# Keys of the cached sequences in pieces of two pages through four slots, 52 units for each sequence, and the sampled rows' pass between the prompt's last units

## The reference

```python
def project(x, w_in, b_f):                 # q, k, v (8 heads of 64), logf, u
    h = jnp.einsum('bsd,dc->bsc', x, w_in)
...
def fox_sample(q, k_new, v_new, logf_new, cache_k, cache_v, cache_logf, page_table):
    k_past = cache_k[page_table].reshape(DB, P, N_HEADS, HEAD_DIM)
    v_past = cache_v[page_table].reshape(DB, P, N_HEADS, HEAD_DIM)
...
    s = jnp.einsum('bqhd,bkhd->bhqk', q, k_all, preferred_element_type=jnp.float32) * HEAD_DIM ** -0.5
    s = s + (Fh[..., P:, None] - Fh[..., None, :])
...
    p = jax.nn.softmax(s, axis=-1)
    out = jnp.einsum('bhqk,bkhd->bqhd', p.astype(v_all.dtype), v_all)
...
def finish(x, attn, pool, w_o, ln1_g, ln1_b, w_gate, w_up, w_down, ln2_g, ln2_b):
    mix = jnp.einsum('bsc,cd->bsd', jnp.concatenate([attn.astype(x.dtype), pool.astype(x.dtype)], axis=-1), w_o)
    x1 = layer_norm(DEEPNORM_ALPHA * x + mix, ln1_g, ln1_b)
    hid = jax.nn.silu(jnp.einsum('bsd,df->bsf', x1, w_gate)) * jnp.einsum('bsd,df->bsf', x1, w_up)
    ffn = jnp.einsum('bsf,fd->bsd', hid, w_down)
    return layer_norm(DEEPNORM_ALPHA * x1 + ffn, ln2_g, ln2_b)
```

## Time and profile before

| | |
|---|---|
| median of three executions | 1519.34 us |
| the profiled execution | 1522.9 us, its span 1520.7 us |
| mean granted clock of TensorE | 0.947 of full |
| TensorE busy | 1384.2 us (91%) |
| VectorE, ScalarE, GpSimd busy | 737.0 (48%), 354.6 (23%), 534.7 us (35%) |
| moved by the DMA engines | 252.90 MB, 166 GB/s in the mean |
| read from HBM | 241.89 MB |

### The profile page before, as it was taken

The page is one execution under the profiler, slowest core; times in us unless marked ns, Lnnn a source line. Parts: engine busy times, 40 slices in busy tenths (PEclk is TensorE's granted clock), DMA queues, the critical chain, the costliest instruction groups (busy, mean ns, idle before and its releaser), DMA issues.

```text
span 1520.7 us, 21098 instructions
## 1 busy us (share of the span) xinstructions
PE 1384.2 (91%) x7585; PEld 1097.4 (72%) x7585; DVE 737.0 (48%) x1014; ACT 354.6 (23%) x514; POOL 534.7 (35%) x203
## 2 busy tenths in 40 slices
PE   7999999999984879999999999999899999998774
PEld 5898989988884867767767677777677777756422
DVE  4745354444659653545354745553554442225702
ACT  3534343533400232021211111212111112112300
POOL 1110000022134327456467365664564652120500
PEclk9999999999997989999999999999999999999756
DMA  7312011010553337666766577666575763424895
GB/s 248 108 56 70 28 57 41 29 49 1 169 191 105 128 116 231 228 199 192 242 191 222 171 246 229 198 225 218 175 230 190 243 248 112 152 106 147 302 347 211
DMA packets 103175, 252.90 MB, mean 166 GB/s; under 512 B 12576, under 2 KB 13985, under 8 KB 97688
## 3 DMA queue, kind: packets, MB, share of 16 engines
q1 hardware_dynamic: 99776, 240.68, 47.7%
q0 software_dynamic: 3296, 10.88, 2.1%
HBM read 241.89 MB, written 9.86 MB: 166 GB/s over the span
## 4 chain that ended last, share of the span: by engine, by line
PE 78%; DVE 10%; DMA 5%; issue 3%; ACT 2%; POOL 1%; SPq 0%; DVEq 0%; ACTq 0%; POOLq 0%
PE PSM L1261 30%; PE PSM L1279 15%; PE PSM L1031 11%; PE PSM L1301 4%; PE PSM L1097 4%; DMA AR<-ws 4%; PE PSM L1044 3%; PE PSM L1083 2%; PE PSM L1207 2%; PE PSM L1350 1%; PE PSM L1363 1%; DVE SC L1600 1%; PE PSM L1240 1%; DMA WR<-xT 1%; PE PSM L1378 1%
## 5 line engine op out<-in xcount | busy, mean ns | idle before, releaser
L681 POOL TENSOR_TENSOR AR<-AR,QB 128x2048 f32<-128x2048 f32 x64 | 300.2, 4699 | 121.7 <-DMA AR<-cache_k 109.1
L688 POOL TENSOR_TENSOR WL<-WR,WH 128x1024 fp32r<-128x1024 f32 x55 | 136.0, 2473 | 336.7 <-ACT WH L899 336.7
L1261 PE MATMUL PSM<-XH,WH 128*128 128x512 f32 x672 | 216.6, 404 | 0.0
L1261 PE MATMUL PSM<-XL,WH 128*128 128x512 f32 x672 | 212.8, 398 | 0.0
L1261 PE MATMUL PSM<-XH,WL 128*128 128x512 f32 x672 | 212.6, 398 | 0.0
L1600 DVE TENSOR_REDUCE SC<-AR 128x32 f32<-128x2048 f32 x64 | 145.8, 2279 | 109.8 <-POOL AR L681 109.8
L1787 DVE TENSOR_TENSOR ACC<-ACC,PSM 128x512 f32<-128x512 f32 x176 | 118.3, 683 | 133.6 <-PE PSM L1279 133.4
L1261 PEld LDWEIGHTS PSM<-XH,WH 128*128 128x128 f32 x672 | 123.4, 189 | 48.8 <-issue 22.2
L899 ACT CAST WH<-WR 128x1024 fp32r<-128x1024 f32 x55 | 57.5, 1047 | 413.6 <-PE PSM L1261 212.0
L1279 PE MATMUL PSM<-R 128*128 128x512 f32 x528 | 150.4, 393 | 0.0
L1261 PEld LDWEIGHTS PSM<-XH,WL 128*128 128x128 f32 x672 | 127.6, 190 | 30.4
(11 more groups left out here) (245 smaller groups left out, 2143.2 us busy)
## 6 DMA issues: line engine op xcount, KB each, us to landing
AR<-cache_k SPq DMA_DIRECT2D x256, 256.0 KB, 3.4
AR<-cache_v SPq DMA_DIRECT2D x256, 256.0 KB, 3.4
AR<-ws SPq DMA_DIRECT2D x37, 1024.0 KB, 7.1
WR<-ffn SPq DMA_DIRECT2D x66, 512.0 KB, 4.3
WR<-w_in SPq DMA_DIRECT2D x16, 512.0 KB, 3.7
WR<-w_o SPq DMA_DIRECT2D x5, 1024.0 KB, 5.1
WR<-xT SPq DMA_DIRECT2D x8, 512.0 KB, 5.6
AR<-negF_d SPq DMA_DIRECT2D x8, 512.0 KB, 3.8
```

Of the source, the lines that this page charges most:

```text
L681: pool.tensor_tensor(keys, keys, QB[:].rearrange("p (o n) -> p o n", o=1).to_broadcast([P, CH, AW]), ALU.mult).then_inc(k_mul, 1)
L688: pool.tensor_tensor(lo, WR[:, raw_weight(e), :], hi.bitcast(F32), ALU.subtract).then_inc(ffn_lo, 1)
L1261: ins = pe.matmul(out[:, hc], (hi, lo)[a][:, k * P:(k + 1) * P], x[b][:, k, hc], start=(k == 0 and n == 0), stop=(k == KC - 1 and n == 2))
```

## The change

Keys come in pieces of two pages (`KP`), 16 for each sequence, through four slots of half the size (`KS`), in the same memory. Multiplications and reductions are by piece, twice as many and half as long. In the output stage reductions stand behind products 8 to 22, and on SyncE four pieces are queued before the fourth load of output weights, and the first four pieces of sequence 1 before the wait for `vs_zero`. The sampled rows are turned before the mixer's last tile, and their mixer columns are made after product 1. Windows have 52 units; the two value slots are refilled at separate units. The sampled rows' layers begin at unit 418. Their G and U tiles are merged: a GU tile holds the same number of bytes, two row chunks for both, and leaves gate and up sums in one PSUM bank, so that one copy by ScalarE and half as many passes of TensorE sum them (with a mask `gumask` of 16 columns). There are 37 tiles as before, spaced 2 or 3 units, the last at 521; the rows' second layer norm stands at units 523 to 525. The FFN of the prompt, its units and the weight tiles are the same.

```diff
+KP = 2
+NKP = NPAGE // KP
+KS = 4
...
-KRED0 = {7: 0, 9: 1, 11: 2, 13: 3, 15: 4, 17: 5, 19: 6, 21: 7}
-WIN = 62
+KRED0 = {8: (0,), 9: (1, 2), 10: (3,)} | {n: (n - 7,) for n in range(11, 23)}
+WIN = 52
...
-VALUES = (9, 24, 39, 54)
-VLOAD = tuple(o + 2 for o in VALUES)
-OWN, COLUMNS, MAXIMUM, KEEP, HEADMAX = 57, 59, 60, 60, 61
-KMUL = (3, 10, 16, 23, 29, 36, 42, 49)
-KRED = tuple(o + 4 for o in KMUL)
-KLOAD = (0, 1) + tuple(o + 1 for o in KRED[:-2])
-ROWMAX, Q_LOAD, G_LOAD = 55, 53, 57
+VALUES = (9, 21, 32, 44)
+VLOAD = tuple(o + n for o in VALUES for n in (1, 4))
+OWN, COLUMNS, MAXIMUM, KEEP, HEADMAX = WIN - 5, WIN - 3, WIN - 2, WIN - 2, WIN - 1
+KMUL = tuple(2 + (WIN - 16) * i // (NKP - 1) for i in range(NKP))
+KRED = tuple(o + 3 for o in KMUL)
+ROWMAX, Q_LOAD, G_LOAD = WIN - 9, KMUL[-1] + 3, WIN - 6
...
+        order += [("GU", g, r) for r in range(parts("GU", g))]
+        order += [("D", g - 1, r) for r in range(parts("D", g - 1))] if g >= 1 else []
+    order += [("D", TGROUPS - 1, r) for r in range(parts("D", TGROUPS - 1))]
+    units = {step: TSTART + 5 * n // 2 + 3 * (n >= parts("GU", 0)) for n, step in enumerate(order)}
+    return units, [units["GU", g, parts("GU", g) - 1] + 2 for g in range(TGROUPS)]
...
+CSPAD = NB * WIN
+MIX, RESID, SQRT1, SCALE1, FACTORS1, OFFSETS1 = (CSPAD + n for n in (2, 11, 12, 13, 14, 18))
+TURN1, TURNED1, TSTART = (CSPAD + n for n in (20, 21, 22))
...
+SUNIT = {("W", n, 0): MIX + 2 * n for n in range(4)} | STEPS_S
+SAMPLE2 = max(SUNIT.values()) + 2
+LNVEC2 = BEGIN["D", NPAIR - 1] - 4
+LAST = max(SAMPLE2 + 5, NORM2 + 2 * RT + 4)
...
-        KR = [AR[:, n * 2 * D:(n + 1) * 2 * D] for n in (0, 1)]
+        KR = [AR[:, n * D:(n + 1) * D] for n in range(KS)]
...
-            first_keys(0)
-            first_keys(1)
+            keys(0)
+            keys(1)
             output_load_raw(2)
             sp.wait_ge(sn_st, 16 * 4)
             sp.wait_ge(ob_free, O["sw"] + 1)
             sp.wait_ge(tb_free, T["un"] + 1)
             sp.dma_start(QB[:], q_d[0:1, :].to_broadcast([P, AW])).then_inc(qb_ld, 16)
+            sp.wait_ge(lnew_done, 1)
+            keys(2)
+            keys(3)
+            output_load_raw(3)
             sp.wait_ge(g_st, 16 * NB)
             sp.dma_start(GB[:].rearrange("p t h -> p (t h)"), G_d[0]).then_inc(gb_ld, 16)
-            output_load_raw(3)
...
+            for n in range(12, NKP):
+                keys(n)
+            sp.wait_ge(k_mul, NKP)
             sp.dma_start(QB[:], q_d[1:2, :].to_broadcast([P, AW])).then_inc(qb_ld, 16)
+            for n in range(NKP, NKP + KS):
+                keys(n)
...
-                for c in range(NCH):
-                    n = (b + 1) * NCH + c
-                    if o == KLOAD[c] and b + 1 < NB:
-                        pages(n, KR, n % 2, t["cache_k"], k_ld, k_red, n - 1)
+                for i in range(NKP):
+                    n = (b + 1) * NKP + i + KS
+                    if o == KRED[i] + 1 and n < NB * NKP:
+                        keys(n)
...
-                    if o == VLOAD[c // 2 - 1] and n < NB * NCH:
+                    if o == VLOAD[c - 2] and n < NB * NCH:
...
             turn_pair(PAIRS - 1)
+            turn_sample(0)
+            turn_sample(1)
...
-                if n in (0, 2):
-                    turn_sample(n // 2)
-                if n == HRT - 1:
+                if n == 0:
                     sample_mixer()
...
-                    rounds = ((r, 0),) if cols == HALF else ((0, 0), (1, 4 * cols))
-                    for k, at in rounds:
+                    rounds, last = (1, 3) if cols == HALF else (2, 1)
+                    for a in range(rounds):
                         for q in range(4):
...
-                if n in (0, 2):
-                    keep_sample(n // 2)
-                if n == HRT + 1:
+                if n == 1:
+                    sample_columns()
                     sample_inputs()
...
+                if u == SAMPLE2:
+                    dve.wait_ge(t_used, len(STREAM))
+                    sample_mean(2, e_var)
+                if u == SAMPLE2 + 2:
+                    sample_scale(2)
+                    dve.wait_ge(e_vec_ld, 32)
+                    sample_factors(e_g1)
+                    dve.wait_ge(e_g1, 2)
+                    sample_offsets(xs2, svec2, e_y)
```

More of the change, by code:

```diff
@@ L138, in sample_steps, with parts @@
 def sample_steps():
[L140 to L141 removed]
     order = []
     for g in range(TGROUPS):
[L145 to L154, removed]
+        order += [("GU", g, r) for r in range(parts("GU", g))]
[3 more added lines that the diff above has]
+    return units, [units["GU", g, parts("GU", g) - 1] + 2 for g in range(TGROUPS)]
+def parts(kind, g):
+    full = 4 * g + 4 <= FT
+    return {"GU": (2, 4), "D": (1, 2)}[kind][full]
+CSPAD = NB * WIN
+MIX, RESID, SQRT1, SCALE1, FACTORS1, OFFSETS1 = (CSPAD + n for n in (2, 11, 12, 13, 14, 18))
+TURN1, TURNED1, TSTART = (CSPAD + n for n in (20, 21, 22))
+STEPS_S, SUMS = sample_steps()
+STREAM = [("W", n, 0) for n in range(4)] + list(STEPS_S)
 TINDEX = {step: n for n, step in enumerate(STREAM)}
[L156 removed]
+SUNIT = {("W", n, 0): MIX + 2 * n for n in range(4)} | STEPS_S
 NORM2 = BEGIN["D", NPAIR - 1] + 2
[L158 removed]
+SAMPLE2 = max(SUNIT.values()) + 2
+LNVEC2 = BEGIN["D", NPAIR - 1] - 4
+LAST = max(SAMPLE2 + 5, NORM2 + 2 * RT + 4)
 def weight_order():
@@ L415, in build @@
         silu_done, gu_done, hh_done, hl_done = sem("silu_done"), sem("gu_done"), sem("hh_done"), sem("hl_done")
-        k_ld = [sem("k_ld0"), sem("k_ld1")]
+        k_ld = [sem(f"k_ld{n}") for n in range(KS)]
         v_ld = [sem("v_ld0"), sem("v_ld1")]
@@ L434, in pages @@
             def pages(n, ring, slot, cache, done, used=None, count=None):
-                numbers = [sp.value_load(page[0:1, bass.ds(n * CH + j, 1)], min_val=0, max_val=POOL_PAGES - 1)
-                           for j in range(CH)]
+                many = KP if ring is KR else CH
+                numbers = [sp.value_load(page[0:1, bass.ds(n * many + j, 1)], min_val=0, max_val=POOL_PAGES - 1)
+                           for j in range(many)]
                 if used is not None:
@@ L526, in _ @@
                 sp.dma_start(ACC[:, i, :], t["x"][i * P:(i + 1) * P, :]).then_inc(x_ld, 16)
[L527 to L530, removed]
+            for n in range(4, 7):
+                keys(n)
             output_load_raw(4)
@@ L533, in _ @@
             weight_tile(0)
-            for n in range(3, NCH):
-                first_keys(n)
+            for n in range(7, 12):
+                keys(n)
             sp.wait_ge(o_free, HRT * OC)
@@ L688, in rest @@
                 pool.tensor_tensor(lo, WR[:, raw_weight(e), :], hi.bitcast(F32), ALU.subtract).then_inc(ffn_lo, 1)
-            for c in range(NCH):
-                multiply(c, 64 * (c // 2 + 1), 16)
+            for n in range(NKP):
+                multiply(n)
             for e in range(2):
@@ L1673, in _ @@
             cat_rows_lo(0, 0)
+            for m in range(2):
+                keep_sample(m)
             mixer_input(0)
-            cat_rows_lo(0, 1)
-            cat_rows_lo(0, 2)
-            mixer_output(0)
-            for r in range(3, KC):
-                cat_rows_lo(0, r)
             dve.wait_ge(ob_full, O["sp"] + 1)
@@ L1690, in _ @@
             dve.tensor_copy(UN, TB[0:STATE, 0:AW]).then_inc(tb_free, 1)
+            cat_rows_lo(0, 1)
+            cat_rows_lo(0, 2)
+            mixer_output(0)
+            for r in range(3, KC):
+                cat_rows_lo(0, r)
             output_lo(1)
@@ L1961 @@
             blkmask[32 * j + h, h] = 1
+    gumask = np.zeros((P, 2 * NB), np.float32)
+    for j in range(4):
+        for b in range(NB):
+            gumask[32 * j + b, NB * (j // 2) + b] = 1
     cum = ((row[:, None] // NPAGE == row[None, :] // NPAGE) & (row[:, None] >= row[None, :])).astype(np.float32)
```

196 lines of the change are left out of this document (94 added, 102 removed).

## The result

The changed kernel takes 1504.1 us (median, 1500.4 to 1510.6) against 1519.1 for the kernel before on the same chip: ratio 0.9899, 95% interval 0.9877 to 0.9921. So it is 1.0% faster, where 3.5% were forecast; 1504 lies above the range of 1446 to 1491. The profiled execution took 1500.7 us, its span is 1498.9, against 1520.7 before and 1467 forecast: **32 us** are to be explained.

What follows compares the result with a forecast made beforehand. TensorE bound the plateau, VectorE 458-496 us, transfers the tail. D10's start 1389.3 + 42 - 3 (W tile's wait) - 20 - 5 + 4 = 1407, plus 60: span 1467, median 1466 us; range 1446 to 1491.

Steps and rivals of the forecast that it cites:

- The tiles, +42: Ahead of the prompt's last down segment: 29 more `ws` tiles at 1.25 us and 5 sums at 1.2, +42 us.
- The stage before the FFN, -20: Output stage and row statistics: four late things removed, less two added costs, -20 us; bounds -8 to -25.
- (d): At unit 8 TensorE waits 7.7 us for XL; sequence 1's keys queued ahead of `vs_zero` bring it earlier, -5 us.
- (a): Before splitting the fourth load of output weights VectorE idles 7.3 us; sampled columns made after product 1 remove it, -7.
- (b): Before the third reduction VectorE idles 8.5 us; four key slots fill that chain before it starts, -8.5.
- (c): VectorE's two-input instructions slowed beside GpSimd's multiplies, three adding 9.9 us; multiplies half as long take half away, -5.
- The denominators, -5: Plateau: TensorE's 13.9 us of waits for denominators shrink with multiplies half as long, -5 us (0 to -10).
- SyncE's queue, +4: In the windows: a few TensorE stalls because SyncE's issue queue has least room, +4 us (0 to +25).
- The 87%: Share of SyncE's queue time that a window's unchanged work would fill in shorter windows: 533 of 620 us.
- rival 1: SyncE's queue binds a little: TensorE waits 2 to 4 us for `cache_v` in each window, 1483 us; chance 0.14.
- the last step: Conversion from span to median: add 2.2 us around the span, subtract 3.6 from profiled execution to median, giving 1466 us.
- The end, 60: From the start of D10 (the prompt's last down segment, units 512 to 527) to the end: 60 us (56 to 66).

Runs made afterwards that it cites:

- the hold: GpSimd's first key multiply waits for VectorE's head splits: 1501.0 us added to the changed kernel, 1461.7 added to it with value loads first and the sampled norm last.

## Why the prediction was wrong

- **The tiles, +42.** Right. Two tiles start 3.98 us apart with two product units between them, and 3.94 with two down units: 1.19 and 1.22 us each. The sum took 0.96. In the changed kernel:

```profile
1251.46 1.06 PE L1380 MATMUL PSM<-AR,GB 128*32 128x512 f32 x8 [1.02 <-DVE GB L1903]
...
1255.44 1.06 PE L1380 MATMUL PSM<-AR,GB 128*32 128x512 f32 x8
...
1285.29 1.06 PE L1367 MATMUL PSM<-AR,GB 128*32 128x512 f32 x8
...
1289.23 1.07 PE L1367 MATMUL PSM<-AR,GB 128*32 128x512 f32 x8
...
1302.49 0.96 PE L1389 MATMUL PSM<-gumask_sb,QB 128*128 128x16 f32 x8
```

- **The stage before the FFN, -20.** It gave 16.3. (d) held: TensorE waits 2.4 us at unit 8 for 7.7. (a) and (b) held in that VectorE no longer stands idle there, but (a) was partly eaten by a lock which I hadn't counted: multiplies now run while the heads are split, 9.30 us for 4.90, as the hold shows. What was late next wasn't VectorE but TensorE itself, busy for 20.00 of 20 us where the first row statistics were due. In the row statistics the longest two-input instruction went from 5.24 to 3.36 us, and the sixteen of this size from 31.9 to 26.3 us in all: (c) gave its 5. The queued pieces held eight splits elsewhere. The Trainium skill (SBUF — State Buffer, section "SBUF: two separate sides") says that GpSimd and a VectorE instruction with two SBUF inputs take the shared port pair as an exclusive lock for the whole instruction. The trace of the splits agrees, 9.30 us for 4.90. What whole pieces of four pages would have cost the splits, no run shows. The window of the changed kernel from 440 to 460 us:

```profile
440.00:460.00 20.00, 20.00 (x172) 20.00 (x171) 15.73 (x22) 0.41 (x2) 9.59 (x5) 1.00 0.74 267
```

- **The denominators, -5.** Under-sized: 11.4. The pieces that are ready ahead, which I feared, cost it nothing that can be seen there.

- **SyncE's queue, +4. This step failed**: it cost 29.7, some 26 us more. The wait is the one that I named as what would show the prediction wrong, at the chunk that I named as tightest. I gave that chunk 5 us to spare, and it came 1.5 to 5.6 us late. The walk went by the times at which slots come free and left out much that stands ahead in the order by then. The 87% was a mean over the window, and I read the rest as room. (Over the five windows from 625 to 1073 us it is 83%, since a window takes 90 us and not 86; the 79% above takes in the last 87 us, in which no keys are loaded.) It isn't room: of the 74 us of waits in these five windows 51 are for reductions, most of them at a window's head, where the next key piece waits for the first reduction, and behind that wait 34 pages go out, the last four of which are the sixth chunk. "A late queue stops waiting" was the reason against rival 1. It is false of this wait: the queue came early to it in each of the four windows shown above, and was late again by the sixth chunk, some 38 us on. Also false was that four slots take the key waits away: 58.7 us of them are left for 60.9, fewer and longer. Rival 1 was the mechanism, in size 29.7 / 7 = 4.2 us a window for its 3. The range took rival 1 in at 1483; what carried the time out of it is the size, 9 us more than rival 1 counted, together with the longer end and the last step below.

- **The end, 60.** It took 67.5. The norm was priced from the earlier trace rows at 8.4, and shown at 9.2. The 3 us off for fewer tiles weren't there: with the norm behind, the last gain ends 50.9 us after D10's start, where it took 48.0 before (1389.2 to 1437.1). VectorE's order is the bound of that stretch, not TensorE, so two tiles less brought nothing there. The last store took 4.7 us to the end instead of 3.5.

- **The last step**, from the profiled execution to the median, took 3.6 off; here the median is 3.4 above the profiled execution. Of the 38 us between 1466 and 1504, 32 are the span's and the other 6 this.

- **No `ws` in the last chain, a clock near 1 to D10**: as said (0.98 from 570 us to D10). A tile lands in 4.9 us for 7.1.

## What to carry to other kernels

In this case a queue's mean load said little. Find the wait at which it starts afresh in each round, count all that stands in its order between that wait and each deadline, and compare that with the time there is; 34 issues of 1.07 us and four tiles didn't fit into the 34 us there were (from 641.8 to a landing wanted at 679.9, less the 4.1 of the transfer), with the queue at 83%. Where one queue refills two kinds of buffers, issue the one that TensorE reads ahead of the one that has slots in hand. An instruction on few rows cost VectorE what one on all 128 did: put such a job behind the last large store, not ahead of it.

## What the runs showed of the hardware

- A page's issue with its number from memory costs SyncE 1.07 us, and 0.6 of this is the register load: the queue worked 492 of 620 us with it and 232 without, for about as many pages (421 and 417).
- Eight two-input splits of VectorE took 9.30 us where multiplies of GpSimd ran beside the first 5.1 us of them, and 4.90 with these held back.
- After waits of 5.6 and 3.5 us TensorE's granted clock was 0.73 and 0.86 over windows of 12 us, for 1.00 just ahead of the second.
- VectorE took 1.21 us for an addition of 8x1024 and as much for one of 128x1024 (1.22), and 0.68 for one of 128x512 (its second operand in PSUM): the partitions cost nothing, the columns all.
